# Recurrence's ends reordered, key pages with halves side by side, last tile's logits early, selection's last round moved

## The chip, the cores and the metric

The kernel runs on one core of one Trainium2 chip, as one program. The metric is the device time of one execution in microseconds; several executions are timed and their median is given. Profiles come from one execution each, taken by the hardware profiler. The engines are TensorE (PE, with its weight loads PEld), VectorE (DVE), ScalarE (ACT), GpSimd (POOL) and SyncE (SP), which only issues transfers here.

## The reference, cut to what matters

One inference step of a two-layer decoder for 512 prompt tokens and 8 samples of 4 tokens. Each layer projects its input into four head groups, joins their outputs in one projection, and adds a mixture of experts. The change touches two of the groups:

```python
# A: sparse attention; an indexer scores all keys, the best topk are kept
score = where(admissible, einsum('bth,bths->bts', wi, relu(dots)), -inf)
_, sel = lax.top_k(score, topk)                  # 128 for prompt rows, 129 for sample rows
logits = einsum('bthd,btkhd->bthk', q, k_sel) * 64 ** -0.5
out = einsum('bthk,btkhd->bthd', softmax(logits), v_sel)
# samples: keys and values of 512 past tokens lie in pages of 128, found by page_table
# B: RWKV-7, state s of 64x64 for each of 4 heads
def step(s, inp):
    r_t, w_t, k_t, v_t, a_t, b_t = inp
    sa = einsum('bhvk,bhk->bhv', s, a_t)
    s = s * w_t + sa[..., None] * b_t + v_t[..., None] * k_t
    return s, einsum('bhvk,bhk->bhv', s, r_t)
# y is then centred and scaled for each head, and gated
```

## The kernel before, in words

Each engine runs its own program, written out by hand, and waits on counting semaphores; the order of the work on an engine is the order in its program. A layer goes through these stages: `projections`, `rwkv`, the attention (`prompt_attention` and `sample_attention` on PE, `attention` on ACT and DVE), `output_projection`, `experts`. All of it is float32. PSUM has 8 banks of 512 columns, `ps[:, bank]`.

The recurrence (`rwkv`) cuts the prompt into 8 chunks of 64 tokens, in two halves g = 0, 1 of four chunks. Nearly all its products are 64x64, two at a time in the two halves of the partitions (helper `diagonal`, line 893, to which the profile puts all of them). PE, DVE and ACT count what they have done in three semaphores, `rw_mm`, `rw_v` and `rw_a`; the lists `RW_PE`, `RW_DVE` and `RW_ACT` name each increment in its order, and `v("t1")` or `mm("h_1")` waits for one by name. At the start PE makes five groups, `bar0 ab0 bar1 ab1 kar0` (`bar` and `kar`: 16 products of 128 columns by `wide`; `ab`: 16 of 64 columns), and DVE masks them with 12 operations of line 2073 (`first`, `keys`). PE waits first for `fm_copied`, ACT's copies of the last projection columns out of banks 2 to 5. Then come squares and inverses of the chunk matrices, with DVE's spare time filled by quarters of the top-k rounds (`select(n)`: quarters 0 and 1 of a round find the maxima of two score chains each, line 2317; quarters 2 and 3 replace them, line 2319).

In the tail PE adds up each half's state growth and its reads (`grown(g)`, `read(g)`, 32 products each) and then goes from chunk to chunk: `step(c)` needs state c - 1 from DVE (`t{c}`), makes state c's sum (`h_{c}`) and the chunk's reads; DVE's `state(c)` (line 2164) scales it. The samples' own short recurrence is spread between: `s_rc`; `s_m`, 4 products of 512 columns; DVE's masking, reduction and `s_w` (lines 2183 and 2187); `s_y`; DVE's `spread(p)`; and `s_t`, 12 products of 512 columns, whose result DVE scales (line 2210). `finish_selection` makes round 16 of the selection and the bias that the attention adds.

When all three counts are full, the attention starts; SP loads the key pages and POOL the value pages, 32 each a layer. PE: sums for the centring of y, gates, `logits(i)` for the four query tiles, `output(i)` (transposes of the probabilities, then products with the values), `sample_logits`. DVE: `y_centred`, `masked(i)` (bias and row maximum), `normed(i)`, `y_rates` and the rest of the output norm. ACT: gate and deviation, `exps(i)`, `turned(i)` (copies of the transposes), copies of the results. `logits(2)` overwrites the banks of `logits(0)` and `logits(1)`, so it waits until `masked(1)` has read them; `logits(3)` waits likewise for `masked(2)`.

## Time and profile before

| | |
|---|---|
| runs timed | 1325.25, 1317.95, 1319.84 us |
| median | 1319.84 us |
| the profiled execution | 1318.73 us |
| its span, first to last instruction | 1317.1 us |
| mean granted TensorE clock | 0.927 |
| PE busy | 86% of the span |
| DVE busy | 49% |
| recurrence of layer 0 | from 221 to 304 us of the span |
| attention of layer 0 | from 304 to 364 us |

The trace numbers microseconds from the span's start. A line number is one of the kernel above; a helper's line stands for all its callers. What stands in square brackets behind a row is how long the engine sat idle before it and who released it. PEclk is the granted clock as a share of 2.4 GHz.

### The profile page before, as it was taken

The page shows a single profiled execution, that of the slowest core. Times are in us where ns is not written, and L with a number is a line of the kernel's source. Part 1 is how long each engine was busy: PE and PEld are TensorE (multiplying, and loading weights), DVE is VectorE, ACT ScalarE, POOL GpSimd, SP SyncE. Part 2 cuts the span into 40 slices and gives each one's busy share as a digit, 9 for nine tenths or more (in the row PEclk, how much of TensorE's full clock was granted, in tenths as well). Part 3 has the DMA queues.
Part 4 walks back from the last instruction along what each step waited for, and adds up shares of the span by engine and source line. Part 5 has one row for each costly group of instructions (what it writes and reads, how often), then busy time and mean ns, then how long its engine had stood idle before and what let it go on. Part 6 is the DMA issues. An engine that isn't in the chain of part 4 may idle for free.

```text
span 1317.1 us, 24577 instructions
## 1 busy us (share of the span) xinstructions
PE 1127.5 (86%) x9786; PEld 685.4 (52%) x9786; DVE 651.4 (49%) x1353; ACT 327.9 (25%) x774; POOL 165.4 (13%) x225
## 2 busy tenths in 40 slices
PE   8999998987899369999599999999778982999940
PEld 4587777973545323332256777889434451333310
DVE  0046898875633611111643588988772453111128
ACT  0234341303421111111244343412053210111100
POOL 0130008105000020000301000450230002000020
PEclk9989999998999679999799999999889985999975
DMA  7199110007660769997522112100296247699742
GB/s 285 56 395 354 48 56 26 7 3 225 208 260 1 319 233 354 423 423 257 203 77 65 57 48 64 33 21 4 64 275 256 101 168 300 245 410 421 300 150 103
DMA packets 66548, 240.37 MB, mean 183 GB/s; under 512 B 8738, under 2 KB 28354, under 8 KB 57026
## 3 DMA queue, kind: packets, MB, share of 16 engines
q1 hardware_dynamic: 46800, 169.15, 33.9%
q0 software_dynamic: 14592, 52.10, 10.9%
q10 hardware_dynamic: 5042, 17.54, 3.3%
q8 instruction: 79, 1.29, 0.4%
q14 instruction: 35, 0.29, 0.1%
HBM read 190.21 MB, written 50.78 MB: 183 GB/s over the span
## 4 chain that ended last, share of the span: by engine, by line
PE 82%; DVE 5%; issue 3%; ACT 3%; DMA 2%; SPq 2%; DVEq 2%; POOL 1%; POOLq 0%; ACTq 0%
PE ps L755 20%; PE ps L1299 13%; PE ps L893 11%; PE ps L1256 8%; PE ps L1314 7%; PE ps L701 4%; PE ps L735 4%; SPq L484 2%; PE ps L815 2%; PE ps L1286 2%; PE ps L1128 1%; PE ps L711 1%; ACT arena L1391 1%; PE ps L1235 1%; PE ps L1223 1%
## 5 line engine op out<-in xcount | busy, mean ns | idle before, releaser
L1391 ACT ACTIVATE arena<-ps 128x512 f32<-128x512 f32 (+14 forms) x342 | 142.3, 454 | 612.4 <-PE ps L755 137.3
L755 PE MATMUL ps<-arena 128*128 128x272 f32 x1088 | 259.7, 397 | 0.0
L755 PEld LDWEIGHTS ps<-arena 128*128 128x128 f32 x1088 | 206.4, 192 | 47.8 <-issue 4.0
L1299 PE MATMUL ps<-arena 128*32 128x512 f32 x1536 | 169.7, 592 | 4.8 <-ACT arena L1391 4.8
L893 PE MATMUL ps<-arena 64*64 64x64 f32 (+3 forms) x4016 | 150.6, 234 | 18.8 <-DVE arena L2164 12.1
L893 PEld LDWEIGHTS ps<-arena 64*64 64x64 f32 x4016 | 137.3, 136 | 31.2 <-issue 18.0
L1256 PE MATMUL ps<-arena 128*128 128x512 f32 x256 | 112.4, 594 | 0.0
L1299 PEld LDWEIGHTS ps<-arena 128*32 128x32 f32 x1536 | 51.3, 110 | 116.9 <-issue 116.9
L1314 PE MATMUL ps<-arena 128*32 128x512 f32 x768 | 87.4, 595 | 3.3 <-DVE arena L2623 2.0
L2617 DVE COPY arena<-ps 128x256 f32<-128x256 f32 x24 | 10.2, 425 | 140.2 <-PE ps L1331 140.2
L1256 PEld LDWEIGHTS ps<-arena 128*128 128x128 f32 x256 | 47.5, 189 | 56.5 <-issue 56.5
L711 PE MATMUL ps<-arena 128*128 128x512 f32 x34 | 23.2, 852 | 49.2 <-DMA rows_in<-arena,ints 37.0
L2623 DVE COPY arena<-ps 128x512 f32<-128x512 f32 x24 | 16.6, 693 | 91.0 <-PE ps L1314 91.0
L701 PE MATMUL ps<-arena 128*128 128x420 f32 (+1 forms) x128 | 52.3, 571 | 5.1 <-DMA arena<-in_xT 5.1
L735 PE MATMUL ps<-arena 128*128 128x512 f32 (+1 forms) x128 | 52.7, 569 | 3.1 <-ACT arena L1696 3.1
L1696 ACT ACTIVATE arena<-ps,arena 128x128 f32<-128x128 f32 (+1 forms) x112 | 38.8, 451 | 58.4 <-PE ps L1223 43.4
L1314 PEld LDWEIGHTS ps<-arena 128*32 128x32 f32 x768 | 23.2, 109 | 50.1 <-issue 47.7
L2307 DVE MATCH_REPLACE8 arena<-arena 32x544 f32<-32x544 f32 (+3 forms) x82 | 47.1, 585 | 0.0
L2300 DVE MAX8 arena<-arena 32x8 f32<-32x544 f32 (+3 forms) x82 | 43.7, 589 | 1.7
L1725 ACT ACTIVATE arena<-ps 128x256 f32<-128x256 f32 x24 | 9.3, 386 | 137.6 <-PE ps L1299 137.6
L701 PEld LDWEIGHTS ps<-arena 128*128 128x128 f32 x128 | 24.9, 196 | 31.8 <-issue 26.7
L711 PEld LDWEIGHTS ps<-arena 128*128 128x128 f32 x34 | 9.2, 281 | 61.9 <-DMA rows_in<-arena,ints 37.3
(348 smaller groups left out, 1333.2 us busy)
## 6 DMA issues: line engine op xcount, KB each, us to landing
arena<-in_w_gu SPq DMA_DIRECT2D x32, 2048.0 KB, 13.8
arena<-in_w_dn SPq DMA_DIRECT2D x32, 1024.0 KB, 14.4
arena<-in_wf SPq DMA_DIRECT2D x34, 512.0 KB, 3.7
rows_in<-arena POOLq DMA_DIRECT2D x12, 1024.0 KB, 25.1
arena<-rows_in SPq DMA_DIRECT2D x24, 512.0 KB, 13.8
rows_out<-arena ACTq DMA_DIRECT2D x24, 512.0 KB, 8.6
arena<-in_cache_v POOLq DMA_DIRECT2D x64, 128.0 KB, 5.7
arena<-in_cache_k SPq DMA_DIRECT2D x64, 128.0 KB, 5.5
```

The lines of the kernel that those rows point to most:

```text
L701: mm = pe.matmul(ps[:, k, 0:w], m.xT[:, c, row_tile(k % NT)], m.wa[:, c, a:a + w], start=c == 0, stop=c == KC - 1, skip_group_check=True)
L711: pe.matmul(ps[:, 7, :], ident, m.consts[:, 0:512], start=True, stop=True)
L735: mm = pe.matmul(ps[:, k % 2, 0:w], m.xT[:, c, row_tile(i)], m.wa[:, c, a:a + w], start=c == 0, stop=c == KC - 1)
L755: mm = pe.matmul(ps[:, 2 + 2 * h + n % 2, 0:HALF], m.wf[n % 3][:, c, :], m.xT[:, c, h * HALF:h * HALF + HALF], start=c == 0, stop=c == KC - 1)
L893: mm = pe.matmul(out[q], lhsT[q], rhs[q], start=start, stop=stop, skip_group_check=check)
L1256: mm = pe.matmul(ps[:, 2 * (i % 2) + h, :], m.yT[:, c, row_tile(i)], m.wout[c // 4][:, c % 4, 512 * h:512 * h + 512], start=c == 0, stop=c ...
L1299: mm = pe.matmul(ps[q, 3 + k, :], m.xgT[:, c, q], m.w_gu[HOME[i]][:, c, :], start=c == 0, stop=c == KC - 1, skip_group_check=True)
L1314: mm = pe.matmul(ps[q, 5 + h, :], m.hT[:, f, q], m.w_dn[HOME[i]][:, f, 512 * h:512 * h + 512], start=f == 0, stop=f == 1, skip_group_check ...
L1391: return act.activation(out, in_, ACT.Copy)
L1696: ins = act.activation(m.xT[:, c, P * i:P * i + n], ps[:, 4 + c // 4, n * (c % 4):n * (c % 4) + n], ACT.Identity, bias=m.lnc[:, 1, c:c + 1 ...
L2300: dve.max(m.top8[c][rows], m.score[c][rows])
L2307: dve.match_replace(m.score[c][rows], m.top8[c][rows], m.score[c][rows], TAKEN)
```

## The change

Four things are changed. At the recurrence's start PE makes `bar0` and `kar0` before it waits for `fm_copied`, and DVE masks in the new order. In the tail the samples' products move between the two halves and between the steps, `step` no longer begins before both halves are grown and read, and DVE's selection quarters move (1 and 3 in place of 4; the last 2 behind the last signal). In the attention `logits(3)` comes before `output(0)`, the two halves of `sample_logits` are split around `output(2)`, `finish_selection` stands between `masked(0)` and `masked(1)`, and `normed(2)` behind `masked(3)`. A key page lies in SBUF with its two halves side by side, so that each partition gets 256 floats in one run instead of twice 128, and the product reads it in four pieces of 128.

```diff
@@ -172,12 +172,12 @@
-RW_PE = counts("bar0 ab0 bar1 ab1 kar0 d2_0 d2t_0 d2_1 d2t_1 kar1 d4_0 d4t_0 d4_1 d4t_1 tb0 tb1 d8_0 d8_1 tv0 tv1 "
+RW_PE = counts("bar0 kar0 ab0 bar1 ab1 d2_0 d2t_0 d2_1 d2t_1 kar1 d4_0 d4t_0 d4_1 d4t_1 tb0 tb1 d8_0 d8_1 tv0 tv1 "
                "x4_0 x4_1 ta0 ta1 x2_0 x2_1 tk0 tk1 x1_0 x1_1 wv0 wv1 xt_0 xt_1 s_bar ft_0 ft_1 s_t s_kar "
-               "z1_0 z1_1 s_d2 z2_0 z2_1 s_z s_wv z3_0 z3_1 s_pp pp0 pp1 gx0 gx1 h0 y0 h1 y1 "
-               "h_1 s_rc h_2 h_3 s_m0 s_m1 h_4 h_5 h_6 s_y h_7 y_7 s_t0 s_t1")
-RW_DVE = counts("q0 dt0 q1 dt1 km0 d2_0 d2_1 km1 d4_0 d4_1 x8_0 x8_1 x4_0 x4_1 x2_0 x2_1 x1_0 x1_1 s_q s_km z1_0 z1_1 s_x "
-                "z2_0 z2_1 s_z z3_0 z3_1 s_pp pp0 pp1 gx0 gx1 t1 t2 s_rc t3 t4 t5 s_w t6 s_u0 t7 s_u1 t8 s_t0 s_t1")
+               "z1_0 z1_1 s_d2 z2_0 z2_1 s_z s_wv z3_0 z3_1 s_pp pp0 pp1 gx0 gx1 h0 y0 s_rc h1 s_m0 s_m1 y1 "
+               "h_1 h_2 h_3 s_y h_4 h_5 s_t0 h_6 s_t1 h_7 y_7")
+RW_DVE = counts("q0 km0 dt0 q1 dt1 d2_0 d2_1 km1 d4_0 d4_1 x8_0 x8_1 x4_0 x4_1 x2_0 x2_1 x1_0 x1_1 s_q s_km z1_0 z1_1 s_x "
+                "z2_0 z2_1 s_z z3_0 z3_1 s_pp pp0 pp1 gx0 gx1 t1 s_rc s_w t2 t3 t4 t5 s_u0 t6 s_u1 t7 s_t0 t8 s_t1")
@@ -358,7 +358,7 @@
     m.s_pTn, m.s_o = ([view(R4 + at + w * k, w) for k in range(2)] for at, w in ((2 * T + 2 * PAST, P), (2368, WA)))
-    m.K = [view(at, 2, 4, PAST) for at in (R2, XT0)]
+    m.K = [view(at, 4, NPAGE, 2, PAGE) for at in (R2, XT0)]
@@ -481,8 +481,8 @@
                 sp.wait_ge(s["state_out"], nth(l, "state_out", 64))
-            sp.dma_start(m.K[g][:, :, j:j + 1, PAGE * c:PAGE * c + PAGE],
-                         din["cache_k"][bass.ds(l * NPHYS + page, 1)].rearrange("z p q k -> p q z k"))\
+            sp.dma_start(m.K[g][:, j, c:c + 1, :, :],
+                         din["cache_k"][bass.ds(l * NPHYS + page, 1)].rearrange("z p q k -> p z q k"))\
@@ -919,14 +919,21 @@
         pe.wait_ge(s["rw_in"], nth(l, "rw_in", 1))
-        pe.wait_ge(s["fm_copied"], nth(l, "fm_copied", NCH))
         pe.wait_ge(s["job_out"], nth(l, "job_out", 12))
-        for g in range(2):
-            wide(2 * g, lambda k: cut(m.BE, g, k), lambda k: both(g, k)).then_inc(s["rw_mm"], 1)
+        def barred(g):
+            return wide(2 * g, lambda k: cut(m.BE, g, k), lambda k: both(g, k))
+        def turned_bar(g):
...
                 mm = diagonal(ps[:, 4 + g, CH * k:CH * k + CH], cut(AE, g, k), cut(m.BE, g, k))
-            mm.then_inc(s["rw_mm"], 1)
+            return mm
+        barred(0).then_inc(s["rw_mm"], 1)
         wide(6, lambda k: cut(m.KE, 0, k), lambda k: both(0, k)).then_inc(s["rw_mm"], 1)
+        pe.wait_ge(s["fm_copied"], nth(l, "fm_copied", NCH))
+        turned_bar(0).then_inc(s["rw_mm"], 1)
+        barred(1).then_inc(s["rw_mm"], 1)
+        turned_bar(1).then_inc(s["rw_mm"], 1)
@@ -1045,10 +1052,6 @@
-        for g in range(2):
-            grown(g).then_inc(s["rw_mm"], 1)
-            read(g).then_inc(s["rw_mm"], 1)
@@ -1063,35 +1066,46 @@
-        v("gx0")
-        step(1)
-        for p in range(2):
-            mm = diagonal(ps[:, 4, NS * p:NS * p + NS], m.sPP[:, p, 1, :], m.sQ[:, p, 1, 0:NS])
-        mm.then_inc(s["rw_mm"], 1)
-        step(2)
-        step(3)
-        v("s_rc")
-        pe.wait_ge(s["state_in"], nth(l, "state_in", 32))
-        for p in range(2):
-            diagonal(ps[:, 5 + p, :], m.sLR[:, p, :], m.TB[:, p]).then_inc(s["rw_mm"], 1)
-        v("gx1")
-        step(4)
-        step(5)
-        step(6)
-        v("s_w")
-        for p in range(2):
-            o = ps[:, 7, CH * p:CH * p + CH]
-            diagonal(o, m.sT[:, 2, p, :], m.sKM[:, p, 1, :], start=p == 0, stop=False, check=True)
-            diagonal(o, m.sPP[:, p, 0, :], m.sQ[:, p, 1, :], start=False, stop=False, check=True)
-            mm = diagonal(ps[:, 7, CH * p:CH * p + NS], m.sW[:, p, :], eye[:, NS:2 * NS], start=False, check=True)
-        mm.then_inc(s["rw_mm"], 1)
-        step(7).then_inc(s["rw_mm"], 1)
-        for p in range(2):
-            v(f"s_u{p}")
+        def sample_rows_out():
+            for p in range(2):
+                o = ps[:, 7, CH * p:CH * p + CH]
+                diagonal(o, m.sT[:, 2, p, :], m.sKM[:, p, 1, :], start=p == 0, stop=False, check=True)
+                diagonal(o, m.sPP[:, p, 0, :], m.sQ[:, p, 1, :], start=False, stop=False, check=True)
+                mm = diagonal(ps[:, 7, CH * p:CH * p + NS], m.sW[:, p, :], eye[:, NS:2 * NS], start=False, check=True)
+            return mm
+        def sample_state(p):
...
             diagonal(o, m.sT[:, 1, p, :], m.VEb[p], start=False, stop=False, check=True)
-            diagonal(o, eye, m.TB[:, p], start=False, check=True).then_inc(s["rw_mm"], 1)
+            return diagonal(o, eye, m.TB[:, p], start=False, check=True)
+        grown(0).then_inc(s["rw_mm"], 1)
+        read(0).then_inc(s["rw_mm"], 1)
+        v("gx0")
+        for p in range(2):
+            mm = diagonal(ps[:, 4, NS * p:NS * p + NS], m.sPP[:, p, 1, :], m.sQ[:, p, 1, 0:NS])
+        mm.then_inc(s["rw_mm"], 1)
+        grown(1).then_inc(s["rw_mm"], 1)
+        v("gx1")
+        v("s_rc")
+        pe.wait_ge(s["state_in"], nth(l, "state_in", 32))
+        for p in range(2):
+            diagonal(ps[:, 5 + p, :], m.sLR[:, p, :], m.TB[:, p]).then_inc(s["rw_mm"], 1)
+        read(1).then_inc(s["rw_mm"], 1)
+        step(1)
+        step(2)
+        step(3)
+        v("s_w")
+        sample_rows_out().then_inc(s["rw_mm"], 1)
+        step(4)
+        step(5)
+        v("s_u0")
+        sample_state(0).then_inc(s["rw_mm"], 1)
+        step(6)
+        v("s_u1")
+        sample_state(1).then_inc(s["rw_mm"], 1)
+        step(7).then_inc(s["rw_mm"], 1)
@@ -1155,34 +1169,34 @@
         logits(2)
+        logits(3)
...
         output(0)
-        logits(3)
         output(1)
-        sample_logits(l)
+        sample_logits(l, 0)
         output(2)
+        sample_logits(l, 1)
...
-    def sample_logits(l):
+    def sample_logits(l, g):
...
         bias = m.bias[3]
...
+        pe.wait_ge((s["k0_in"], s["k1_in"])[g], nth(l, f"k{g}_in", 256))
+        a = 2 - 2 * g
+        pe.wait_ge(s["qb_ready"], nth(l, "qb_ready", 1))
+        pe.wait_ge(s["lg_taken"], nth(l, "lg_taken", 4))
+        for j in range(4):
             for p in range(2):
-                pe.matmul(ps[:, a + 1, 0:NS], m.QB[:, p, 4 * g:4 * g + 4, :].rearrange("p b m -> p (b m)"), m.kT[:, p, SEQ:T],
-                          start=p == 0, stop=False)
-            pe.matmul(ps[:, a + 1, 0:NS], spread[0:NS, P * g:P * g + P], bias[0:NS, PAST:T], start=False, stop=True)\
-                .then_inc(s["s_lg_mm"], 1)
+                pe.matmul(ps[32 * j:32 * j + 32, a, :].rearrange("m (c k) -> m c k", c=NPAGE), m.QB[:, p, 4 * g + j, :], m.K[g][:, j, :, p, :],
+                          start=p == 0, stop=False, skip_group_check=True)
+        pe.matmul(ps[:, a, :], spread[0:NS, P * g:P * g + P], bias[0:NS, 0:PAST], start=False, stop=True,
+                  skip_group_check=True)
+        for p in range(2):
+            pe.matmul(ps[:, a + 1, 0:NS], m.QB[:, p, 4 * g:4 * g + 4, :].rearrange("p b m -> p (b m)"), m.kT[:, p, SEQ:T],
+                      start=p == 0, stop=False)
+        pe.matmul(ps[:, a + 1, 0:NS], spread[0:NS, P * g:P * g + P], bias[0:NS, PAST:T], start=False, stop=True)\
+            .then_inc(s["s_lg_mm"], 1)
@@ -1647,6 +1661,11 @@
+        def sample_logits(g):
+            act.wait_ge(s["s_lg_mm"], nth(l, "s_lg_mm", g + 1))
+            copy(m.s_lg[g][:, 0:PAST], ps[:, 2 - 2 * g, :])
+            copy(m.s_lg[g][:, PAST:T], ps[:, 3 - 2 * g, 0:NS]).then_inc(s["s_lg"], 1)
@@ -1655,12 +1674,10 @@
         exps(3)
-        for g in range(2):
-            act.wait_ge(s["s_lg_mm"], nth(l, "s_lg_mm", g + 1))
-            copy(m.s_lg[g][:, 0:PAST], ps[:, 2 - 2 * g, :])
-            copy(m.s_lg[g][:, PAST:T], ps[:, 3 - 2 * g, 0:NS]).then_inc(s["s_lg"], 1)
+        sample_logits(0)
...
         output(2)
+        sample_logits(1)
@@ -2082,13 +2099,15 @@
-        def first(g):
+        def near(g):
...
+        def turned(g):
@@ -2106,9 +2125,11 @@
         dve.wait_ge(s["ln_done"], nth(l, "ln_done", 0))
-        first(0)
-        first(1)
+        near(0)
         keys(0)
+        turned(0)
+        near(1)
+        turned(1)
@@ -2166,18 +2187,11 @@
         state(0)
-        select(4)
-        mm("h_1")
-        state(1)
+        select(1)
...
             .then_inc(s["rw_v"], 1)
-        mm("h_2")
-        state(2)
-        mm("h_3")
-        state(3)
-        mm("h_4")
-        state(4)
+        select(3)
@@ -2186,29 +2200,37 @@
         dve.drain().then_inc(s["rw_v"], 1)
-        mm("h_5")
-        state(5)
+        for c in range(1, 4):
+            mm(f"h_{c}")
+            state(c)
...
             own = m.const("s_rows").unsqueeze(2).broadcast_to([P, DB, CH])
-            tt(m.sW[:, p, :], m.sW[:, p, :], m.sPP[:, p, 0, :], add)
-            dve.drain()
...
-        select(2)
-        mm("s_y")
-        spread(0)
-        mm("h_6")
-        state(6)
-        spread(1)
-        mm("h_7")
-        state(7)
-        finish_selection()
-        for p in range(2):
+        def sample_out(p):
...
+        mm("s_y")
+        tt(m.sW, m.sW, m.sPP[:, :, 0, :], add)
+        mm("h_4")
+        state(4)
+        dve.drain()
+        spread(0)
+        mm("h_5")
+        state(5)
+        spread(1)
+        mm("h_6")
+        state(6)
+        sample_out(0)
+        mm("h_7")
+        state(7)
+        sample_out(1)
+        select(2)
+        dve.drain()
@@ -2367,11 +2389,14 @@
         y_centred(l)
-        for i in range(3):
-            masked(i)
-        for i in range(3):
-            normed(i)
+        masked(0)
+        finish_selection()
+        masked(1)
+        masked(2)
+        normed(0)
+        normed(1)
         masked(3)
+        normed(2)
```

## Rows read from the trace of the kernel before

**Rows 1.** The page: busy time of the engines; the ended-last chain by line.

```profile
PE 1127.5 (86%) x9786; PEld 685.4 (52%) x9786; DVE 651.4 (49%) x1353; ACT 327.9 (25%) x774; POOL 165.4 (13%) x225
...
PE ps L755 20%; PE ps L1299 13%; PE ps L893 11%; PE ps L1256 8%; PE ps L1314 7%; PE ps L701 4%; PE ps L735 4%; SPq L484 2%; PE ps L815 2%; PE ps L1286 2%; PE ps L1128 1%; PE ps L711 1%; ACT arena L1391 1%; PE ps L1235 1%; PE ps L1223 1%
```

**Rows 2.** That chain in order of time, layer 0: start, us, what.

```profile
217.47 3.55 issue
221.02 63.22 PE ps L893 x1864
```

**Rows 3.** Timeline of the recurrence: start, us, engine, line, operation; idle before, releaser.

```profile
224.65 6.56 DVE L2073 TENSOR_TENSOR arena<-ps,arena 128x512 f32<-128x512 f32 x12 [3.67 <-PE ps L893]
...
260.33 0.60 ACT L1391 ACTIVATE arena<-ps 128x512 f32<-128x512 f32 x1 [0.33 <-PE ps L893]
...
272.22 0.60 ACT L1391 ACTIVATE arena<-ps 128x512 f32<-128x512 f32 x1 [1.16 <-PE ps L893]
...
866.24 6.56 DVE L2073 TENSOR_TENSOR arena<-ps,arena 128x512 f32<-128x512 f32 x12 [2.14 <-PE ps L893]
```

**Rows 4.** Windows, layer 0: length; PE, PEld, DVE, ACT, POOL busy; PEclk; DMA, GB/s.

```profile
222.00:222.50 0.50, 0.50 (x8) 0.50 (x6) 0.00 (x0) 0.00 (x0) 0.50 (x1) 0.50 0.00 0
...
297.00:299.00 2.00, 2.00 (x8) 0.60 (x6) 1.75 (x6) 0.17 (x1) 0.00 (x0) 0.50 0.00 0
...
326.00:329.00 3.00, 3.00 (x8) 0.88 (x6) 0.00 (x0) 0.19 (x1) 0.00 (x0) 0.50 1.10 317
```

**Rows 5.** Timeline of the recurrence's tail, layer 0.

```profile
277.58 0.29 DVE L2164 TENSOR_TENSOR arena<-ps,arena 128x128 f32<-128x128 f32 x1 [0.45 <-PE ps L893]
...
280.40 2.09 DVE L2317 MAX8 arena<-arena 128x8 f32<-128x512 f32 x4
...
284.60 2.87 PE L893 MATMUL ps<-arena 64*64 64x64 f32 x40 [0.16 <-DVE arena L2164]
...
287.49 1.28 DVE L2183 TENSOR_TENSOR arena<-ps,arena 128x512 f32<-128x512 f32 x2
...
288.85 1.94 DVE L2187 TENSOR_REDUCE arena<-arena 128x64 f32<-128x512 f32 x2
...
291.25 1.38 PE L893 MATMUL ps<-arena 64*64 64x64 f32 x40 [2.93 <-DVE arena L2164]
...
295.40 7.70 PE L893 MATMUL ps<-arena 64*64 64x64 f32 x40 [2.78 <-DVE arena L2164]
...
296.97 0.70 DVE L2300 MAX8 arena<-arena 32x8 f32<-32x544 f32 x1
...
300.68 0.17 DVE L2330 TENSOR_TENSOR arena<-arena 32x32 f32<-32x32 f32 x1
...
303.16 0.69 DVE L2210 TENSOR_TENSOR arena<-ps,arena 128x512 f32<-128x512 f32 x1 [1.54 <-PE ps L893]
```

**Rows 6.** Timeline of the attention, layer 0, by engine.

```profile
306.45 1.29 DVE L2218 SCALAR_TENSOR_TENSOR arena<-ps,arena 128x512 f32<-128x512 f32 x2 [2.60 <-PE ps L1101]
...
310.65 1.22 DVE L2352 TENSOR_TENSOR arena<-ps,arena 128x1024 f32<-128x1024 f32 x1
...
314.85 1.76 DVE L2356 TENSOR_TENSOR arena<-ps,arena 128x1536 f32<-128x1536 f32 x1 [1.66 <-PE ps L1120]
...
322.28 0.42 ACT L1391 ACTIVATE arena<-ps 128x128 f32<-128x128 f32 x2
...
325.70 3.78 PE L1120 MATMUL ps<-arena 64*128 64x512 f32 x8
...
346.88 0.74 ACT L1666 ACTIVATE arena<-arena 128x544 f32<-128x544 f32 x1
...
348.98 1.09 PE L1128 MATMUL ps<-arena 128*64 128x128 f32 x8 [1.39 <-ACT arena L1391]
```

**Rows 7.** Timeline, layer 0: SP's key pages, and the first products that read them.

```profile
305.91 27.98 SPq L484 DMA_DIRECT2D arena<-in_cache_k  x32
...
333.61 1.95 PE L1177 MATMUL ps<-arena 128*32 128x512 f32 x16
```

More of the change, by code:

```diff
@@ L1064, in step @@
             return mm
+        def sample_rows_out():
[6 more added lines that the diff above has]
+        def sample_state(p):
+            o = ps[:, 4 + p, :]
+            diagonal(o, m.sT[:, 0, p, :], m.UEb[p], start=True, stop=False, check=True)
+            diagonal(o, m.sT[:, 1, p, :], m.VEb[p], start=False, stop=False, check=True)
+            return diagonal(o, eye, m.TB[:, p], start=False, check=True)
+        grown(0).then_inc(s["rw_mm"], 1)
+        read(0).then_inc(s["rw_mm"], 1)
         v("gx0")
-        step(1)
         for p in range(2):
@@ L1157, in prompt_attention @@
         logits(2)
+        logits(3)
         pe.wait_ge(s["yn_std"], nth(l, "yn_std", 1))
         output(0)
-        logits(3)
         output(1)
-        sample_logits(l)
+        sample_logits(l, 0)
         output(2)
+        sample_logits(l, 1)
         output(3)
-    def sample_logits(l):
+    def sample_logits(l, g):
         spread = m.const("spread")
         bias = m.bias[3]
-        for g in range(2):
-            pe.wait_ge((s["k0_in"], s["k1_in"])[g], nth(l, f"k{g}_in", 256))
-            a = 2 - 2 * g
-            pe.wait_ge(s["qb_ready"], nth(l, "qb_ready", 1))
-            pe.wait_ge(s["lg_taken"], nth(l, "lg_taken", 4))
-            for j in range(4):
-                for p in range(2):
-                    pe.matmul(ps[32 * j:32 * j + 32, a, :], m.QB[:, p, 4 * g + j, :], m.K[g][:, p, j, :],
-                              start=p == 0, stop=False, skip_group_check=True)
-            pe.matmul(ps[:, a, :], spread[0:NS, P * g:P * g + P], bias[0:NS, 0:PAST], start=False, stop=True,
-                      skip_group_check=True)
-            for p in range(2):
-                pe.matmul(ps[:, a + 1, 0:NS], m.QB[:, p, 4 * g:4 * g + 4, :].rearrange("p b m -> p (b m)"), m.kT[:, p, SEQ:T],
-                          start=p == 0, stop=False)
-            pe.matmul(ps[:, a + 1, 0:NS], spread[0:NS, P * g:P * g + P], bias[0:NS, PAST:T], start=False, stop=True)\
-                .then_inc(s["s_lg_mm"], 1)
@@ L1657, in attention @@
         exps(3)
-        for g in range(2):
-            act.wait_ge(s["s_lg_mm"], nth(l, "s_lg_mm", g + 1))
-            copy(m.s_lg[g][:, 0:PAST], ps[:, 2 - 2 * g, :])
-            copy(m.s_lg[g][:, PAST:T], ps[:, 3 - 2 * g, 0:NS]).then_inc(s["s_lg"], 1)
+        sample_logits(0)
         turned(2)
         output(2)
+        sample_logits(1)
         for g in range(2):
```

3 lines of the change are left out of this document (removed).

## The prediction

> **What bounds the kernel now.** I read the page first. TensorE (PE) is busy 86% of the span, VectorE (DVE) half of it, and the chain that ended last is almost all PE lines [rows 1]. So a change pays only where PE waits on the chain, or where PE runs at the lower of its two clock levels. Next I read the chain in order of time and looked in the two stages that the diff touches, the recurrence and the attention, which come once in each of the two layers. Three places show waits.
>
> The first is the start of the recurrence. PE stands still for 3.55 us before its first product at 221.02 [rows 2]. The code waits there for `fm_copied`, the copies of the last projection columns by ScalarE (ACT). The clock then drops: at 222 PE runs at 0.50, that is 1.2 instead of 2.4 GHz [rows 4]. DVE, idle too, gets its first mask 3.67 us after it was free; in layer 1, 2.14 us after [rows 3].
>
> The second is the tail. From the first grown state (277.58) to the last product (303.16 + 0.69) 26.3 us pass [rows 5]. PE idles 2.93 us before 291.25, because DVE's sample sums and a reduction delay state 5, and 2.78 us before 295.40, because DVE runs selection and spreading ahead of state 6 [rows 5]. After that the clock is at 0.50 while the largest products run [rows 4].
>
> The third is the attention. `output(0)` waits for the copy at 322.28, behind all exponentials of tiles 0 to 2, and `logits(3)` then takes 3.78 us between `output(0)` and `output(1)`, at clock 0.50 [rows 4, 6].
>
> **Prices.** A square of 16 products of 64x64 takes 0.93 us (0.60 + 0.33, ACT's rhythm behind it), a wide one with 128 columns 1.76 (0.60 + 1.16) [rows 3]. So one small product costs 58 ns; `grown` or `read` of one half (32) 1.87, one `step` (8) 0.47, half of that until its state can be taken. The 2.87 us at 284.60 hold two steps and the four 512-column products of `s_m`: 1.93, or 0.48 each [rows 5]. The twelve of `s_t` then cost 5.8 at the full clock. On DVE a state is 0.29, two products over 512 columns 1.28, the reduction 1.94, a replace quarter of selection 1.27 ((280.40 - 277.87) / 2), a maximum quarter 1.05 [rows 5].
>
> **Part 1, the start.** `bar0` and `kar0` (2 x 1.76 = 3.5 us, banks that the column copies don't use) move ahead of the `fm_copied` wait and fill the 3.55 us; the other three groups (3.6) then run from 221.0 at the full clock to 224.6. DVE can start its 12 masks (6.56 us) when it is free, 3.67 us earlier in layer 0 and 2.14 in layer 1 [rows 3]. The last of them releases `d2_1` on PE, and PE is ready before that: 224.6 plus a square pair of 1.86 is 226.5, against 221.0 + 6.56 = 227.5 for the mask. So DVE's gain is what counts: 3.67 + 2.14 = 5.8. Behind it PE runs on with no gap to 284 (63.22 us in one piece [rows 2]), so the lead is kept. Bounds: 2 x 2.14 = 4.3 if the low clock comes anyway, 6.7 if all 3.55 + 3.19 of waits vanish in full (the second one less sure); I take 5.8.
>
> **Part 2, the tail.** The work is the same; its order is new. Counted from the end of `grown(0)`: PE does `read(0)`, `s_rc`, `grown(1)` until 4.0, `s_m` until 5.9, `read(1)` until 7.8, `step(1)` until 8.2. DVE meanwhile does one quarter of selection, `s_rc` at 2.4, three quarters until 5.8 (1.27 + 2.09), the sample products until 7.1, the reduction until 9.2, state 1 at 9.5. So here PE waits 1.3 us, where before it waited 2.93. Steps 2 and 3 go round PE and DVE at 0.6 each: 10.7. `s_y` (1.38 of the row at 291.25 less a step, 0.9) and step 4: 11.8. DVE spreads the first sample (1.28) until 13.5; PE has done step 5 by 12.6 and waits 0.9. `s_t0` until 16.4, step 6 until 16.9, `s_t1` until 19.8, step 7 until 20.2; DVE takes state 7 and then the last sample product (0.69) until 21.0. That is 26.3 - 21.0 = 5.3 a layer, say 5.4. DVE's two quarters of selection that now come after the last signal hide under the centring's sums: the centring waited 2.60 us for PE [rows 6], and two quarters are 2 x 1.27 = 2.5. Without that cover they would cost 2.5.
>
> Bounds: PE's own work without any wait ends at 17.4, plus about 0.9 for the last state and product: gain 8.0. If the twelve products of `s_t` fall to the low clock, 5.8 us more: gain -0.4. Before, the clock fell after two waits of 2.9 and 2.8 us close together; the new waits are 1.3 and 0.9. That is nearer to the clock holding, and I take 5.4.
>
> **Part 3, the attention.** Two moves work against each other. Selection's end (296.97 to 300.85, 3.9 us [rows 5]) was hidden under PE's `s_t`; it now stands on DVE before `masked(1)`, and queued behind it are `masked(1)`, `masked(2)` and the first `normed`. On the clock of before, `masked(1)` moves from 310.65 to 314.6 and frees the banks for `logits(2)` at 315.8; that takes about 1.7 us (six eighths of the 3.78 / 2 of `logits(3)`, plus fill). `masked(2)` starts at 317.6, not at 314.85 [rows 6]. Its row maximum comes 2.75 us later, at 321.2; ACT is then free, so the last four exponentials (2.4 us) end at 323.6 and the copy that gates `output(0)` is 1.35 us late. In return `logits(3)` runs from 319.4 in PE's idle time and its 3.78 us leave the chain: +2.4. Later, `output(3)` waits for ACT as before (1.39 us at 348.98, behind two exponentials of 0.74 [rows 6]), but the copy of the second sample logits now stands in that row too (0.60 [rows 3]): -0.6. Net +1.8 a layer. Bounds: 0.4 if `logits(2)`, now between two idle stretches, runs at 0.50 and takes 1.4 longer; 3.3 if `output(0)`, 3.1 us long at 0.50 before (322.6 to 325.7), runs in half of that. I take 1.7, by the clock of the rows and a little for the longer queue.
>
> **Part 4, key pages.** The 32 page loads take SP 27.98 us from 305.91, and PE starts on the first half at 333.61 with no wait before it [rows 7]. In the new order the second half is asked for behind `output(2)`, later than before, so even an unchanged load is in time: 0. The strided moving operand is also priced at 0: the wide products already read their right side in two pieces, and they cost 1.76 for twice the columns of 0.93. Upper bound: the 16 products double, 1.95 x 4 = 7.8 us for the run.
>
> **Sum.** 5.8 + 2 x 5.4 + 2 x 1.7 = 20.0. The profiled execution took 1318.7 (span 1317.1 and 1.6 around it), which gives 1298.7; the median of the runs shown, 1319.84, lies 1.1 above it. I forecast 1299 us.
>
> **Rivals.**
> A. TensorE's clock falls in the tail. For it: `s_t` ran mostly at 0.50 before, and new small gaps stand ahead of it. Against: the gaps are shorter. Half of `s_t` at the low level costs 2.9 a layer: 1305; all of it 1310. Chance 0.18.
> B. Selection's end sits wholly on the path: DVE, not ACT, sets `output(0)`, and the copy is late by all of 3.9 instead of 1.35, 2.55 more a layer: 1304. Against: ACT's exponentials of tiles 0 and 1 run under it. 0.06.
> C. Key pages are worth what the chain shows. It puts 2% of the span, some 26 us, on SP's page issues [rows 1]; a quarter of it saved is 6 us: 1293. Against: PE had no wait there, the loads only tie with PE. 0.05. The Trainium skill, in DMA: Bandwidth & Descriptors (Specifications), puts the smallest piece that moves at line rate at 512 B, and these pieces have that size already. By that rule longer pieces bring nothing and the sum stays; no run here has another piece size to compare.
> D. The change does not do what it says: the tail's order only trades one DVE wait for another and the attention's two moves cancel, so that the start alone pays: 1318.7 - 5.8 = 1313. 0.07.
> E. Slower: the key pages' four-piece moving operand. Its place is the 16 products of each sample half (1.95 us, four times a run). To undo 20.0 us each must cost 5.0 more, 3.6 times its time; beyond that the kernel is slower, at five times (4 x 7.8 = 31.2) 1330. Against it stand the wide products. 0.04.
>
> **How the numbers follow.** The forecast has 0.60, with 1294 to 1303 as its own range. Range for 8 in 10: 1292, just under C, to 1308, which takes in B, half of A and the bound of the strided operand; outside stay D, E and the worse half of A. A change of 0.5% (6.6 us) is about what a measurement here can tell from none: faster than 1313.2 in all of the forecast, A, B, C and a little of D, 0.91; the same in most of D and some of E, 0.06; slower 0.03.
>
> **What would show it.** Part 1: no wait of 3 us before the first product of the recurrence, clock 1.00 there, DVE's first mask within 0.3 us of its last scan product, all masks done 3.4 to 3.8 us earlier in layer 0. Part 2: about 21 us from the first state to the last sample product, PE waits under 1.5, clock 1.00 over `s_t`. Part 3: `masked(2)` 2.7 us later against the recurrence's end, `logits(3)` before `output(0)`, the first copy 1.3 late, about 2.4 gained at the first sample logits. Part 4: fewer packets on SP's queue and no PE wait for pages. It is wrong if the clock is at 0.50 over `s_t`, or if PE waits for DVE in the attention longer than for ACT.

## The result

| | before | changed | ratio, 95% interval |
|---|---|---|---|
| first set, median | 1322.16 us (4 runs) | 1307.76 us (1303.67 to 1310.25) | 0.9884 [0.9851, 0.9917] |
| second set, median | 1324.13 us (17 runs) | 1305.73 us (1301.90 to 1307.90) | 0.9859 [0.9828, 0.9891] |
| profiled execution, span | 1317.1 us | 1306.9 us, second set 1300.2 us | |

The kernel became faster by 15 us (11 to 20) in the first set and 19 (14 to 23) in the second. One of the 17 runs of before, 1349.55 us, is in a slower state that some executions show, and the ratio leaves it out. The forecast was 1299 us, from a gain of 20.0 taken off the profiled execution of before.

To see where the time went, the span is cut in each layer at three places that any kernel here has: the end of the last projection column (L755 in all), the attention's first product (L1099 of before, L1113 after), and the first product of the output projection, which ends the attention (L1245, L1259). All three are times on TensorE (PE); the recurrence runs from the first to the second, the attention from the second to the third.

| us, from the profile | recurrence, layer 0 | layer 1 | attention, layer 0 | layer 1 | all the rest |
|---|---|---|---|---|---|
| before | 86.53 | 84.70 | 60.01 | 60.19 | 1025.67 |
| changed, first set | 76.71 | 76.48 | 59.40 | 62.99 | 1031.32 |
| changed, second set | 76.70 | 77.02 | 60.27 | 60.55 | 1025.66 |

So the recurrence gained 18.0 us (17.5 in the second set) where the prediction had 16.6, and the attention, which should have gained 3.4, lost 2.2 (0.6). The rest, whose code is the same, was 5.6 us longer in one execution and equal in the other. These are single executions, one for each row.

**The recurrence.** The chain of waits of the changed kernel, layer 0 (start, duration, what); against [rows 2] the 3.55 us of standing still are gone:

```profile
215.68 3.68 PE ps L893 x63
...
219.44 5.27 DVE arena L2090 x10
...
225.70 48.11 PE ps L893 x1488
...
285.23 6.09 PE ps L893 x48
```

The same stage by stretches (columns as in [rows 4]): the start, and the products `s_t`. PEclk is 1.00 in all of them; in [rows 4] it was 0.50 at both places.

```profile
216.00:222.00 6.00, 6.00 (x130) 5.91 (x128) 5.66 (x11) 1.40 (x6) 3.99 (x7) 1.00 0.25 90
222.00:226.00 4.00, 3.39 (x108) 3.12 (x106) 4.00 (x8) 0.60 (x1) 3.85 (x3) 1.00 0.02 4
...
284.00:288.00 4.00, 3.29 (x34) 1.41 (x34) 2.58 (x5) 0.21 (x2) 0.00 (x0) 1.00 0.02 4
288.00:292.00 4.00, 3.53 (x46) 1.65 (x41) 1.54 (x4) 0.42 (x1) 0.00 (x0) 1.00 0.00 0
```

PE's waits in the tail: 1.26, 0.17, 0.16 and 0.70 us in place of 2.93 and 2.78 [rows 5].

```profile
280.99 0.68 PE L893 MATMUL ps<-arena 64*64 64x64 f32 x16 [1.26 <-DVE arena L2185]
281.84 1.85 PE L893 MATMUL ps<-arena 64*64 64x64 f32 x56 [0.17 <-DVE arena L2185]
283.85 0.68 PE L893 MATMUL ps<-arena 64*64 64x64 f32 x16 [0.16 <-DVE arena L2185]
285.23 6.30 PE L893 MATMUL ps<-arena 64*64 64x512 f32 x56 [0.70 <-DVE arena L2210]
```

**The attention.** PE in layer 0 of the changed kernel (first set), to be read against [rows 6]:

```profile
304.28 1.80 PE L1134 MATMUL ps<-arena 64*128 64x384 f32 x8 [2.46 <-DVE arena L2374]
307.94 3.78 PE L1134 MATMUL ps<-arena 64*128 64x512 f32 x8 [1.86 <-DVE arena L2378]
...
312.50 0.43 PE L1142 MATMUL ps<-arena 128*64 128x128 f32 x2 [0.16 <-ACT arena L1405]
...
318.50 1.95 PE L1191 MATMUL ps<-arena 128*32 128x512 f32 x16
...
331.40 1.09 PE L1153 MATMUL ps<-arena 128*128 128x128 f32 x8
334.36 1.97 PE L1142 MATMUL ps<-arena 128*64 128x128 f32 x8 [1.87 <-ACT arena L1405]
336.26 1.12 PE L1153 MATMUL ps<-arena 128*128 128x128 f32 x4
337.31 1.97 PE L1142 MATMUL ps<-arena 128*64 128x128 f32 x8
...
339.97 1.85 PE L1142 MATMUL ps<-arena 128*64 128x128 f32 x16
```

Counted from the attention's first product (292.38; in the kernel before 304.00), the first product with values starts at 20.12 against 18.59 before, and the first sample logits at 26.12 against 29.61 [rows 7], so 3.5 us are won by then. Most of that is gone after `output(3)`. Its wait for ScalarE (ACT) is 1.87 in place of 1.39 us, and its products take 1.97 instead of 1.09 us [rows 6]; layer 1 and the second profile show the same two numbers. The stretches before, in and behind that wait have the clock at 1.00, 0.70 and 0.50:

```profile
326.00:332.00 6.00, 6.00 (x43) 3.44 (x42) 2.42 (x2) 1.37 (x3) 0.00 (x0) 1.00 1.03 415
332.00:334.00 2.00, 0.49 (x5) 0.25 (x3) 1.68 (x2) 1.94 (x7) 0.00 (x0) 0.70 0.99 426
334.00:338.00 4.00, 3.64 (x15) 2.98 (x16) 3.77 (x5) 1.38 (x3) 0.00 (x0) 0.50 0.67 272
```

### The profile page after: what moved, and what is told of

Its sections match the earlier page's. It is cut to its first block, busy times and chain, and to the rows that moved or that the text cites. A ratio compares the mean times of both kernels' runs of the same rounds, so it can differ in the third digit from the quotient of the medians.

```text
span 1306.9 us, 24571 instructions
## 1 busy us (share of the span) xinstructions
PE 1129.7 (86%) x9786; PEld 687.4 (53%) x9786; DVE 650.7 (50%) x1351; ACT 328.0 (25%) x774; POOL 166.4 (13%) x225
## 3 DMA queue, kind: packets, MB, share of 16 engines
q1 hardware_dynamic: 38608, 169.15, 33.8%
## 4 chain that ended last, share of the span: by engine, by line
PE 75%; DVE 11%; DVEq 3%; issue 3%; DMA 3%; ACT 3%; POOL 1%; POOLq 0%; ACTq 0%; SPq 0%
PE ps L755 16%; PE ps L1313 13%; PE ps L893 9%; PE ps L1270 8%; PE ps L1328 7%; PE ps L735 4%; PE ps L701 4%; PE ps L1142 2%; PE ps L1300 2%; ACT arena L1405 1%; POOL rows_in L661 1%; PE ps L815 1%; DVE arena L2329 1%; PE ps L1237 1%; PE ps L1249 1%
## 5 line engine op out<-in xcount | busy, mean ns | idle before, releaser
L755 PE MATMUL ps<-arena 128*128 128x272 f32 x1088 | 260.2, 398 | 0.0
L755 PEld LDWEIGHTS ps<-arena 128*128 128x128 f32 x1088 | 206.4, 191 | 48.2 <-issue 4.0
L893 PE MATMUL ps<-arena 64*64 64x64 f32 (+3 forms) x4016 | 146.1, 231 | 5.5 <-DVE arena L2185 3.2
L1270 PE MATMUL ps<-arena 128*128 128x512 f32 x256 | 112.4, 594 | 0.0
L2642 DVE COPY arena<-ps 128x256 f32<-128x256 f32 x24 | 10.2, 425 | 140.2 <-PE ps L1345 140.2
L1270 PEld LDWEIGHTS ps<-arena 128*128 128x128 f32 x256 | 47.5, 189 | 56.6 <-issue 56.5
L711 PE MATMUL ps<-arena 128*128 128x512 f32 x34 | 20.0, 749 | 49.5 <-DMA rows_in<-arena,ints 37.0
L2648 DVE COPY arena<-ps 128x512 f32<-128x512 f32 x24 | 16.6, 693 | 91.1 <-PE ps L1328 91.1
L701 PEld LDWEIGHTS ps<-arena 128*128 128x128 f32 x128 | 24.8, 194 | 31.7 <-issue 26.5
## 6 DMA issues: line engine op xcount, KB each, us to landing
arena<-in_w_dn SPq DMA_DIRECT2D x32, 1024.0 KB, 14.4
rows_in<-arena POOLq DMA_DIRECT2D x12, 1024.0 KB, 25.1
```

The costliest lines, as they stand in the source:

```text
L701: mm = pe.matmul(ps[:, k, 0:w], m.xT[:, c, row_tile(k % NT)], m.wa[:, c, a:a + w], start=c == 0, stop=c == KC - 1, skip_group_check=True)
L755: mm = pe.matmul(ps[:, 2 + 2 * h + n % 2, 0:HALF], m.wf[n % 3][:, c, :], m.xT[:, c, h * HALF:h * HALF + HALF], start=c == 0, stop=c == KC - 1)
L893: mm = pe.matmul(out[q], lhsT[q], rhs[q], start=start, stop=stop, skip_group_check=check)
L1270: mm = pe.matmul(ps[:, 2 * (i % 2) + h, :], m.yT[:, c, row_tile(i)], m.wout[c // 4][:, c % 4, 512 * h:512 * h + 512], start=c == 0, stop=c ...
```

## The experiments

All were run beside the kernel before on the same chip, in three sets on three chips; the gain in microseconds is one minus the ratio, times that set's median of before. The changed kernel's second run shared a set with the last three rows only (`before, ACT's order` to `the same, waits filled`), so the other versions are compared with it by their ratios to before. The stage columns are cut as above, two layers each, from one profile a kernel.

| kernel | median, us | ratio to before | gain, us | recurrence | attention | rest |
|---|---|---|---|---|---|---|
| start alone | 1312.54 | 0.9926 [0.9909, 0.9944] | 9.8 | 82.03, 81.53 | 59.97, 59.87 | 1027.5 |
| tail alone | 1314.94 | 0.9953 [0.9933, 0.9973] | 6.2 | 80.79, 78.85 | 62.59, 62.60 | 1026.2 |
| attention's order alone | 1322.03 | 0.9993 [0.9967, 1.0019] | 0.9 | 88.51, 85.82 | 59.11, 59.42 | 1024.6 |
| key pages alone | 1320.36 | 0.9991 [0.9975, 1.0006] | 1.2 | 88.39, 85.73 | 58.73, 60.04 | 1025.3 |
| changed, old attention order | 1307.27 | 0.9866 [0.9835, 0.9897] | 17.8 | 76.70, 76.35 | 61.31, 61.28 | 1029.2 |
| changed, wait filled | 1302.42 | 0.9834 [0.9803, 0.9866] | 22.0 | 76.72, 76.36 | 58.87, 59.59 | 1024.0 |
| changed, ACT's order | 1298.18 | 0.9797 [0.9760, 0.9834] | 26.9 | 76.72, 76.34 | 57.74, 58.71 | 1029.6 |
| changed, selection's end split | 1303.72 | 0.9844 [0.9811, 0.9876] | 20.7 | 76.70, 76.49 | 59.24, 60.29 | 1025.4 |
| before, ACT's order | 1321.73 | 0.9983 [0.9959, 1.0007] | 2.3 | 87.18, 86.99 | 61.96, 57.72 | 1026.3 |
| changed, ACT's order and split | 1301.10 | 0.9817 [0.9784, 0.9850] | 24.2 | 76.71, 76.48 | 56.97, 57.49 | 1032.3 |
| the same, waits filled | 1299.18 | 0.9804 [0.9772, 0.9836] | 26.0 | 76.70, 76.70 | 58.22, 56.63 | 1029.4 |

**The start alone.** Only the parts of the diff at the recurrence's start: `near` and `turned` on DVE, `barred` and `turned_bar` on PE, and the first names of the two lists.

> The kernel before with the start of the recurrence alone in its new order. Theory 1 (the start pays what the sum says): 4.3 to 5.8 us faster, because the wait ahead of the first product in each layer (3.55 and 3.19 us) goes; the first product of each recurrence has no wait of more than 1 us ahead of it and the clock is 1.00 there. Theory 2 (the missing part of the gain was missing here: what is won at the start is lost again behind it, by a lower clock in the square chain or in the mixture of experts): under 2 us faster, although the wait is gone.

The gain is 9.8 us (7.4 to 12.0), more than theory 1 has. The wait is gone and the clock behind it is 1.00 (the start of layer 0, then of layer 1):

```profile
216.00:220.00 4.00, 4.00 (x81) 3.89 (x82) 3.66 (x6) 1.39 (x6) 2.30 (x4) 1.00 0.44 135
...
858.00:862.00 4.00, 4.00 (x81) 3.98 (x82) 3.67 (x7) 1.40 (x6) 2.16 (x5) 1.00 0.44 133
```

The old start costs differing amounts. In the profile of before the clock behind it is at 0.50 for 3.4 us in layer 0 [rows 4] and not at all in layer 1. In the kernel with the key pages alone, whose start is the same, it is so for 6.8 us and 3.4 us:

```profile
220.00:224.00 4.00, 3.59 (x36) 3.62 (x38) 0.36 (x1) 0.31 (x2) 3.17 (x5) 0.50 0.00 0
...
865.00:869.00 4.00, 4.00 (x66) 4.00 (x67) 0.64 (x2) 0.00 (x0) 3.56 (x6) 0.65 0.00 0
```

There DVE's waits for its first masks are longer too, against 3.67 and 2.14 in [rows 3]:

```profile
224.22 2.55 DVE L2073 TENSOR_TENSOR arena<-ps,arena 128x512 f32<-128x512 f32 x5 [3.86 <-PE ps L893]
227.77 3.98 DVE L2073 TENSOR_TENSOR arena<-ps,arena 128x512 f32<-128x512 f32 x7 [1.00 <-PE ps L893]
...
868.36 6.56 DVE L2073 TENSOR_TENSOR arena<-ps,arena 128x512 f32<-128x512 f32 x12 [3.55 <-PE ps L893]
```

With old start and old tail the recurrence takes 86.5 to 88.5 us in layer 0 and 84.7 to 87.0 in layer 1 over four kernels; the profile of before has the shortest of each. Against the mean of the four (87.65 and 85.81) the start alone is worth 5.6 + 4.3 = 9.9 us, which is what the runs show; against the profile of before 7.7. Not all of it is won at the start. The product that stands at 284.60 in [rows 5], 67.13 us behind the last projection column, comes 63.12 us behind it with the start alone:

```profile
279.14 2.87 PE L893 MATMUL ps<-arena 64*64 64x64 f32 x40 [0.16 <-DVE arena L2175]
```

That is 4.0 us, and 2.75 in layer 1: 6.8 of the 7.7 (8.4 of the 9.9 against the four). The other 0.9 (1.5) come behind that product, in a tail whose code is the old one; why is not shown.

**The tail alone.** Only the parts of the diff in PE's and DVE's tail, with selection's end moved along, since its old place is gone:

```diff
         for i in range(3):
             masked(i)
+            if i == 0:
+                finish_selection()
```

> The kernel before with the tail of the recurrence alone in its new order, selection's end moved behind the first masking of the attention with it; the attention's products stay in their old order. Theory 1 (the tail pays 5.4 a layer and selection's end costs the attention what the prediction gave, 1.35 at the first copy and some 1.4 more at the third tile): 6 to 9 us faster. Theory 2 (selection's end stands on the path in full, 3.9 us a layer): 2 to 4 us faster. In the trace, state 1 to last sample product falls from 26.3 to about 21 us by both.

6.2 us (3.6 to 8.9), by theory 1. Against the profile of before the recurrence is 5.7 and 5.9 us shorter, and the attention gives back 2.6 and 2.4. There the first product with values starts at 21.25 instead of 18.59: `logits(2)`, between two waits, runs at the low clock and takes 2.93 us:

```profile
310.36 2.93 PE L1127 MATMUL ps<-arena 64*128 64x384 f32 x8 [2.47 <-DVE arena L2360]
...
319.71 0.69 PE L1135 MATMUL ps<-arena 128*64 128x128 f32 x2 [1.10 <-ACT arena L1398]
```

**The attention's order alone.** Only the parts of the diff in `prompt_attention`, `sample_logits`, ACT's copies and `normed(2)`, without selection's end.

> The kernel before with the attention's order alone changed: the last tile's logits ahead of the first output, the sample logits split around the third output, ScalarE's copies and the third normalising with them; selection's end stays in the recurrence, where TensorE hides it. Theory 1 (the order pays, only selection's end takes it back): 5 to 7 us faster (2.4 of the logits and 1.35 less 0.6 a layer). Theory 2 (the order itself brings TensorE's clock down later, over the last output, and gives the gain back there): within 2 us of the kernel before, with clock 0.50 over the last tile's products, which take about 1.97 us instead of 1.09.

0.9 us (-2.5 to 4.4): theory 2. The first sample logits start 25.62 us behind the attention's start, 4.0 sooner than before; `output(3)` then takes it back:

```profile
343.67 1.97 PE L1128 MATMUL ps<-arena 128*64 128x128 f32 x8 [1.87 <-ACT arena L1391]
345.57 1.12 PE L1139 MATMUL ps<-arena 128*128 128x128 f32 x4
346.62 1.97 PE L1128 MATMUL ps<-arena 128*64 128x128 f32 x8
...
349.49 1.85 PE L1128 MATMUL ps<-arena 128*64 128x128 f32 x16
```

From 343.67 to the last head's products at 349.49 it is 5.8 us. In the kernel before these steps took 3.2, from 348.98 [rows 6] to this row:

```profile
352.20 1.85 PE L1128 MATMUL ps<-arena 128*64 128x128 f32 x16
```

**Key pages alone.**

> The kernel before with the layout of the key pages alone changed. Theory 1 (the loads are hidden and the four-piece moving operand costs nothing): within 1.5 us, with 8192 packets fewer on the queue and the sample logits' products at 1.95 us as before. Theory 2 (the operand in four pieces is slower, and this is what the whole change lacks): 3 to 8 us slower, each product of the sample logits longer by that. Theory 3 (shorter transfers help the loads that share the queues): 2 to 6 us faster.

1.2 us (-0.8 to 3.3): theory 1. The prediction found no run with another piece size; here the pieces are twice as long. The queue has 38608 packets in place of 46800, the products of the sample logits stay at 1.95 us, and the issues are quicker, 21.46 us for 32 in place of 27.98 [rows 7]; nothing waited for them:

```profile
307.18 21.46 SPq L484 DMA_DIRECT2D arena<-in_cache_k  x32
```

**The old attention order in the changed kernel.** `logits(3)` again behind `output(0)`, both `sample_logits` ahead of `output(2)`, ACT and `normed` accordingly.

> The changed kernel with the attention's products, ScalarE's copies and the normalisings in the order of before; selection's end stays behind the first masking. Theory 1 (the new order is worth nothing once the clock is counted): within 2 us of the changed kernel, attention about 62.6 us in both layers. Theory 2 (the order is worth what the prediction gave it, 2.4 less 0.6 a layer and more): 3 to 6 us slower than the changed kernel.

1307.27 us, between the two medians of the changed kernel: theory 1. The attention is 61.3 in both layers (62.6 was expected), with 1.40 us of wait and full clock at `output(3)`:

```profile
339.31 1.09 PE L1142 MATMUL ps<-arena 128*64 128x128 f32 x8 [1.40 <-ACT arena L1405]
```

So neither alone nor in the whole does the new order pay. Over all the profiles with ACT's old order and nothing put into the wait, `output(3)` is passed 18 times. In the ten passes with a wait of 1.4 us the products behind it run at full clock. In the eight with 1.87 (the changed kernel twice, the attention's order alone and, below, selection's end split) the clock falls to 0.50, in one of them only after the first 1.09 us of products.

**The wait filled.**

```diff
+                if h == 1 and i == 3:
+                    pe.wait_ge(s["s_lg"], nth(l, "s_lg", 1))
+                    for _ in range(3):
+                        pe.matmul(ps[:, 3, :], ident, m.consts[:, 0:512], start=True, stop=True)
```

> The changed kernel with three discarded products of 512 columns (some 1.8 us of TensorE, results read by nobody) put into TensorE's wait for ScalarE inside the last output. Theory 1 (the wait of 1.87 us there lets TensorE's clock fall, and the low clock over the last tile's products costs about 2.6 us a layer): the products with the values stay at 1.09 us at clock 1.00, the attention is 2 to 3 us a layer shorter than in the changed kernel, total 1302 to 1305. Theory 2 (the clock falls for what came long before this wait): the clock is at 0.50 there all the same and the time is that of the changed kernel, or longer by up to 1 us a layer.

1302.42 us: theory 1 by the total and by the clock. The discarded products (L1158) stand where PE waited, and what follows runs at full speed:

```profile
330.72 1.09 PE L1153 MATMUL ps<-arena 128*128 128x128 f32 x8
331.65 2.74 PE L1158 MATMUL ps<-arena 128*128 128x512 f32 x6
334.32 1.09 PE L1142 MATMUL ps<-arena 128*64 128x128 f32 x8
335.34 0.66 PE L1153 MATMUL ps<-arena 128*128 128x128 f32 x4
335.93 1.09 PE L1142 MATMUL ps<-arena 128*64 128x128 f32 x8
```

Filling the wait is all that the edit does there, so the low clock over `output(3)` comes from the wait. The trace shows this, not the total, whose interval overlaps with the changed kernel's. The attention is 3.9 us shorter in both layers together than in the first profile of the changed kernel and 2.4 than in the second, where 4 to 6 were expected.

**ACT's order.**

```diff
         for g in range(2):
+            turned(3, (2 * g, 2 * g + 1))
             act.wait_ge(s["s_max"], nth(l, "s_max", g + 1))
...
-        turned(3)
```

> The changed kernel with ScalarE's copies of the last tile's turned probabilities put between the two exponentials of the samples, two before the first and two before the second, instead of behind both. Theory 1 (ScalarE's order there makes the wait, and the wait brings the clock down): the wait of 1.87 us falls under 1 us, the clock stays at 1.00, the attention is 2.5 to 4 us a layer shorter, total 1300 to 1304. Theory 2 (the clock falls anyway): 1 us a layer at most, total 1305 to 1308.

1298.18 us, a little below theory 1's range. The attention is 5.9 and 4.4 us shorter in both layers together than in the two profiles of the changed kernel (5 to 8 were expected). The wait is 0.25 us:

```profile
333.47 1.09 PE L1153 MATMUL ps<-arena 128*128 128x128 f32 x8
334.81 1.09 PE L1142 MATMUL ps<-arena 128*64 128x128 f32 x8 [0.25 <-ACT arena L1405]
335.83 0.65 PE L1153 MATMUL ps<-arena 128*128 128x128 f32 x4
336.42 1.09 PE L1142 MATMUL ps<-arena 128*64 128x128 f32 x8
...
341.05 0.63 PE L1209 MATMUL ps<-arena 128*128 128x128 f32 x4 [1.17 <-DVE arena L2412]
```

The last row shows what the edit does not win: the samples' attention now waits 1.17 us for DVE, where the changed kernel had no wait.

**The same edit in the kernel before.**

> The kernel before with the one edit to ScalarE's order that was put into the changed kernel before (the last tile's copies between the samples' exponentials). There the wait ahead of the last output is 1.39 us and the clock over its products is 1.00 already. Theory 1 (the edit is worth the wait that it takes away, and gains more in the changed kernel only by the clock): about 1.1 us of attention a layer, 1 to 3 us in all. Theory 2 (ScalarE's order by itself is worth what it brought the changed kernel): 6 us or more.

2.3 us (-0.9 to 5.4): theory 1. The wait of 1.39 goes to 0.25 here too, and in layer 1 the attention is 2.5 us shorter. In layer 0 it is 2.0 longer: the second half of the key pages, in the old layout, came too late once, and its products ran at the low clock behind that wait:

```profile
336.00 3.63 PE L1177 MATMUL ps<-arena 128*32 128x512 f32 x16 [1.15 <-DMA arena<-in_cache_k]
```

**Selection's end split.** `finish_selection` in three pieces: the biases of chains 2 and 1 behind `masked(0)`, that of chain 0 behind `masked(2)`, round 16 and the sample bias behind `normed(1)`.

> The changed kernel with selection's end cut in pieces: the biases of the middle two tiles are made ahead of the second masking, that of the last tile behind the third, the sample chain's last round and bias behind the second normalising. Theory 1 (selection's end on the path costs 1.5 us a layer at the first copy): the first products with values start 18.6 us behind the attention's start instead of 20.1, total 2 to 4 us below the changed kernel. Theory 2 (TensorE then idles longer ahead of the first output and the clock falls over it): the first copy is earlier by that much, but the first sample logits are not, and the total is that of the changed kernel within 1.5 us.

1303.72 us, 2 to 4 below the changed kernel with intervals that overlap, so the runs leave it unclear. The trace is nearer to theory 2: the first product with values is at 18.60 in both layers, but `logits(3)` runs partly at the low clock (3.30 us in layer 0), in layer 1 the first output does, the first sample logits come at 25.70 and 27.80 (26.12 to 28.81 in the changed kernel), and the attention takes 59.24 and 60.29.

**Both, and both with the waits filled** (three discarded products ahead of `logits(3)`, three behind it, two in `output(0)`).

> The changed kernel with both edits that helped it: the last tile's copies between the samples' exponentials, and selection's end in pieces. Theory 1 (the two add up, since one takes a wait at the last output and the other 1.5 us at the first copy): 1294 to 1298, attention 55 to 57 us a layer where the clock holds. Theory 2 (the earlier logits only give TensorE longer waits ahead of the first output, and the clock falls there): as with ScalarE's order alone, 1297 to 1300.

> The kernel with both edits, and eight discarded products of 512 columns in TensorE's three waits around the last logits and the first output (three, three and two; results read by nobody). Theory 1 (the low clock over the logits and the first outputs comes from these waits): clock 1.00 from the attention's start to its end, the last logits at 1.99 us and the first output at full speed in both layers, 2 to 6 us below the kernel with both edits alone. Theory 2 (the discarded products stand in the way): the same or up to 3 us slower.

The two edits make the attention 56.97 and 57.49, the shortest pair without fillers, but the total, 1301.10, is above what either theory had and not below ACT's order alone: the rest took 1032.3 in the profiled execution. With fillers the total is 1.9 us lower with intervals that overlap, so the runs leave it unclear. `logits(3)` takes 1.99 us in both layers, and the clock is 1.00 throughout in layer 1, as theory 1 has it, and up to the samples' values in layer 0. There it falls instead, over products that take 1.94 elsewhere:

```profile
341.30 3.54 PE L1220 MATMUL ps<-arena 128*32 128x256 f32 x32 [0.83 <-ACT arena L1409]
```

The three versions of the changed kernel with ACT's order have overlapping intervals. All three beat the kernel before. Of the two that shared a set with the changed kernel, the filled one has all six runs below the changed kernel's fastest, the other four of six. ACT's order alone is the smallest edit; it ran in another set, and its interval overlaps a little with that of the changed kernel's second set (0.9760 to 0.9834 against 0.9828 to 0.9891).

**The changed kernel again.**

> The changed kernel once more, to stand beside the other kernels of this set and to see what its stretches outside the recurrence and the attention take in another execution. Theory 1 (the stretches outside, 5.6 us longer in the first profile of the changed kernel than in that of before, differ from one execution to the next and not by the change): they come out anywhere between those of the kernels run so far, 1024 to 1031 us; the total is 1305 to 1310. Theory 2 (the change lengthens them): 1030 us or more again.

1305.73 us and a rest of 1025.66: theory 1.

## Why the prediction came out as it did

The time, 1307.76, lies at the upper end of the range, 0.2 us inside it. Two things make up the 8.8 us to 1299. The sum was set against the profiled execution, 1318.7, and the median of before beside the changed kernel was 1322.16: 3.4. The gain between medians was 14.4 and not 19.7 (1318.7 less 1299): 5.3. In the profiles the gain of 10.2 instead of 20.0 is made of 1.4 more in the recurrence, 5.6 less in the attention and 5.6 less in the rest. That the time stayed in the range is partly luck: the start won more than its term and so covered some of what the attention lost, and the second set, with a rest as short as before, lies 2 us lower.

**The start was mis-sized, low.** The step took DVE's gain alone, 5.8. The order of events was right: no wait, the first masks at 0.26 us instead of 3.67 and 2.14, no gap until 273.8. What it missed has three parts, by the start alone. Up to the tail the new start is 4.0 and 2.75 us ahead of the profile of before, 6.8 where 5.8 was forecast: beside the waits, the twelve masks themselves took 6.20 us instead of 6.56. Another 0.9 came in the tail. And the waits of 3.67 and 2.14 are those of one profile with a short stretch of low clock behind the old wait: the prediction saw that stretch in [rows 4] and left it out of the sum, but it already lengthens the 3.67 of layer 0, and in other executions it lasts longer or comes in layer 1 as well. So it is 7.7 us by the two profiles and 9.8 by the runs.

**The tail was right.** From the first state to the last sample product 20.5 us (271.76 to 292.24) where 21 was forecast, with waits of 1.26 and 0.70 where 1.3 and 0.9 were. By difference from the start alone it is 5.3 and 5.1 us a layer for the forecast 5.4. Rival A, the clock falling over `s_t`, is out: 1.00 in both layers.

**The attention failed**, at the step "`output(3)` waits for ACT as before [...] -0.6". The wait itself grew as forecast, by 0.5. What the step lacked is the clock behind it: at 1.39 us before, the products ran at full speed; with 1.87 in the new order they run at 0.50, and the steps up to the last head's products take 2.4 to 2.6 us more (5.6 in layer 0 of the changed kernel, 5.8 with the order alone, 3.2 before). The fillers and ACT's order show it: with the wait filled or at 0.25 us the clock stays at 1.00 there. It is rival A's mechanism at another place. The other two terms held, give or take what the clock does over the logits between two waits (the lower bound of that part) or, in layer 1 of the first profile, over the first outputs. The first copy is 1.3 to 2.7 us late for the forecast 1.35, and short of rival B's 3.9. At the first sample logits 3.5 us are won in layer 0 and 0.8 in layer 1, in the second execution 2.7 and 2.4, where 2.4 was forecast. So 2.4 less 0.5 less 2.5 is about -0.6 a layer; measured were 0.6 and -2.8 in one execution, -0.3 and -0.4 in the other, for the forecast 1.7. The sign that the prediction named, a longer wait for DVE than for ACT, does not decide it: PE's waits, from the one ahead of the attention's first product on, add up to 5.2 us for DVE and 5.1 for ACT in layer 0 of the first profile, and to 6.0 each in layer 1.

**The key pages were right** at 0; rivals C and E fall with it, at 1.2 us (-0.8 to 3.3) and 1.95 us a group as before. The reason given, that the loads only tie with PE, has a limit: when PE came to the second half 33.3 us into the attention in the kernel before with ACT's order, it waited 1.15 us for loads of the old layout.

**Rival D is out**: start and tail each pay. The parts run alone add up to 9.8 + 6.2 + 0.9 + 1.2 = 18.1 us, against 15.3 and 18.7 for the whole.

What stays open is the rest of the kernel. Stretches of untouched code are now and then at the low clock, such as a first block of the experts in the first profile of the changed kernel:

```profile
469.23 8.78 PE ps L1313 x64
```

In the other profile of the same kernel this block takes 7.09. In the nine profiles with the new start the rest is 1024.0 to 1032.3 us, in the five with the old one 1024.6 to 1026.3. The long ones go with the clock: in the six profiles with a rest of 1027.5 us or more it is at 0.50 for 155.5 to 161.7 us of the rest, in the eight others for 147.4 to 154.6. All six have the new start. Whether the new start favours this, or chance did, these profiles can't tell; one or two profiles for each kernel are too few.

## What to carry to other kernels

Price a wait of the busiest engine twice: the wait, and what the engine runs behind it at the lower clock; here a wait that grew by 0.5 us cost 2.4 to 2.6 us more behind it. A product moved into idle time pays only if the next wait on its engine doesn't grow, so look at the queue of the engine that releases it: here, in the changed kernel, one reordering on ScalarE took 4 to 6 us off the attention's two layers, and the whole reordering of the products was worth 0.9 us alone. In the kernel before, where the clock held over `output(3)`, the same edit on ScalarE was worth 2.3. And set a forecast against the median of many executions, stage by stage, since a single profile may hold the shortest pass of a stage.
